# Delta rule: states decayed by ScalarE ahead of time, update products added four heads at once

## The chip, the cores and the metric

One core of one Trainium2 chip runs the kernel. The metric is device time in microseconds (us) of one execution. Engines are named by the profile's letters where rows are meant: PE is TensorE, DVE is VectorE, ACT is ScalarE, POOL is GpSimd, SP is SyncE.

## The reference, cut to what matters

The program computes two transformer-like blocks for 1024 tokens of width 1024. The change lies in the first block, in its bidirectional gated delta rule (4 heads, head size 128, chunks of 64 tokens, so 16 chunks in each direction). Per chunk and head a 128x128 state is read, and then replaced:

```python
def step(state, inp):
    q_i, k_i, u_i, w_i, g_i, a_i = inp
    v_new = u_i - jnp.einsum('bhcd,bhde->bhce', w_i, state)
    o = (jnp.einsum('bhcd,bhde->bhce', q_i * jnp.exp(g_i)[..., None], state)
         + jnp.einsum('bhcs,bhse->bhce', a_i, v_new))
    g_last = g_i[..., -1]
    k_dec = k_i * jnp.exp(g_last[..., None] - g_i)[..., None]
    state = state * jnp.exp(g_last)[..., None, None] + jnp.einsum('bhcd,bhce->bhde', k_dec, v_new)
    return state, o
```

The last but one line is what the change touches: the product of the state with its decay, and the addition of the update product.

## The kernel before, in words

The delta rule runs in one stage (`nc.Block(name="delta_and_window")`) together with the windowed attention of the same block. Both directions go side by side: forward chunk n and backward chunk 15 - n are one step n, each on half of the 128 partitions of a bank. `state` holds 8 states of 128x128 (4 heads, 2 directions) in SBUF; `chunk_decay` holds their decays, one number for each state and chunk.

**Periods and slots.** The order on every engine is written out by hand: the stage is a loop over periods s = 0 to 17, each of 10 slots k = 0 to 9. In a period, step n = s - 2 of the recurrence is done, and beside it parts of a triangular inverse for later chunks (`CHAIN`: `corner_sum`, `inv_sum` on TensorE with `corner_mask`, `inv_add` on VectorE). Of the recurrence in period s:

- slot 0: TensorE multiplies keys and queries with the old states (`state_sums`, L1203, 32 matmuls, into the banks `value_bank` and `kvb[0]`); ScalarE scales the second product (`q_state_scale`, L1382); VectorE subtracts the first (`subtract_state`, L1567).
- slot 4: TensorE forms v_new (`v_sum`, L1214), ScalarE copies it to SBUF (`v_copy`, L1391).
- slot 7: TensorE forms the update products of both directions (`kv_sum`, L1226, into `kvb[0]` and `kvb[1]`); VectorE replaces the states of one direction (`advance(z, 0)`, L1577).
- slot 8: output product (`out_sum`, L1235) and its addition on VectorE (`out_add`, L1585).
- slot 9: VectorE replaces the states of the other direction (`advance(z, 1)`, L1577) and posts the semaphore `s_st`, for which the next period's `state_sums` waits; then it takes up the next chunk (`scores_of`, L1514), whose product (`gram`, L1166) TensorE forms at the end of the period.

**The window attention** fills the slots 1 to 9 (from period 2, slot 4 on) with a running list of steps for 32 units u (`WINDOW_STEPS`): `score u+1`, `turn0 u`, `turn1 u`, `values u`, and again. Four kinds of steps over nine slots a period shift the list by one from period to period, so that slot 1 holds, period after period, `turn0`, `turn1`, `values`, `score`, `turn0`, and so on. In these steps TensorE transposes the probabilities of two heads through one bank `ptb` (L1288), ScalarE copies the first head's out (`copy_turned`, L1428), VectorE the second's (L1676); TensorE's `turn1` waits for ScalarE's copy. ScalarE also forms the probabilities of the next unit (`probs`, L1420) when slot `turn1` comes, and copies the values out of the last quarter of `ptb` after `values` (`copy_out`, L1433); TensorE's `turn0` of the next unit waits for that copy. `score` (L1274) needs no ScalarE instruction. In the last periods ScalarE has squares and scalings of finished outputs in the same slots (L1033, L1473).

Every engine works through its own list in order, so an instruction that waits holds up all behind it.

The function that the change alters, before:

```python
for h in range(DN_HEADS):
    j = d * 4 + h
    ins = nc.vector.scalar_tensor_tensor(state[:, j, :], state[:, j, :], chunk_decay[:, j, c:c + 1],
                                         kvb[hf][:, h, :], ALU.mult, ALU.add)
if hf:
    ins.then_inc(s_st, 1)
```

Of the kernel before, what the change touches and what calls it, by code (L numbers as in the profile page):

```python
# [10 lines left out]
ALU = mybir.AluOpType  # L11
ACT = mybir.ActivationFunctionType
# [11 lines left out]
DN_HEADS, DN_DIM, DN_TAPS, CH = 4, 128, 5, 64  # L24
NCH = SEQ // CH
# [111 lines left out]
def build(nc, t):  # L137

    ctx = ExitStack()
    with ctx:  # L140
        def sb(name, shape, dt=F32, where=ctx, side="left"):
            return where.enter_context(nc.sbuf_tensor(name, shape, dt, side=side))

        def bank(name, shape=(P, HALF), where=ctx):
            return where.enter_context(nc.psum_tensor(name, list(shape), F32))

        def sem(name):
            return ctx.enter_context(nc.semaphore(name))
# [155 lines left out]
        chunk_decay = sb("chunk_decay", [P, 8, NCH], F32, stDN)  # L304
# [48 lines left out]
        s_xturn, s_hhi, s_xcopy = sem("x_turned"), sem("h_hi_ready"), sem("x_copied")  # L353
        s_hlo = sem("h_lo_ready")
        s_sq, s_sqadd = sem("squares_ready"), sem("squares_added")
        s_ss, s_ln, s_rs = sem("square_sums"), sem("log_ready"), sem("rs_ready")
        s_tap, s_conv = sem("taps_step"), sem("conv_sum_ready")
        s_silu_free, s_zsilu = sem("tap_sum_free"), sem("gate_silu_done")
        s_resid_sp = sem("resid_spilled")
# [26 lines left out]
        with blockA as block:  # L386
# [304 lines left out]
            def _(dve):  # L691
# [106 lines left out]
                for c in range(C1):  # L798
# [44 lines left out]
                    elif c == 24:  # L843
# [15 lines left out]
        late = const("late").rearrange("p (r n) -> p r n", r=2)  # L859
        LEVELS, LOWER = 6, CH // 2  # L860
        PAIR_BUFS, INV_BUFS = 4, 3
        pair_keys = sb("pair_keys", [P, PAIR_BUFS, DN_HEADS, 2, CH], F32, stS)
        k_dec = sb("k_dec", [P, 2, DN_HEADS, DN_DIM], F32, stS)
        corner = sb("corner", [P, LEVELS, DN_HEADS, CH], F32, stS)
# [4 lines left out]
        state = sb("state", [P, 8, DN_DIM], F32, stS)  # L869
        tri = [bank(f"tri{i}", where=stS) for i in range(2)]  # L870
        value_bank = bank("value_bank", (P, DN_HEADS, DN_DIM), stS)
        kvb = [bank(f"kvb{i}", (P, DN_HEADS, DN_DIM), stS) for i in range(2)]
# [35 lines left out]
        s_vsum, s_vnew, s_osum, s_kv, s_st, s_o = (sem("v_new_summed"), sem("v_new_then_parts_taken"), sem("out_summed"),  # L908
                                                   sem("kv_summed"), sem("state_ready"), sem("out_stored"))
# [17 lines left out]
        def side(n, hf):  # L927

            return (n, 0) if hf == n % 2 else (NCH - 1 - n, 1)
# [26 lines left out]
        def chain_step(s, k):  # L956

            kind, behind, lv = CHAIN[k]
            n = s - behind
            return (kind if 0 <= n < NCH else None), n, lv  # L960

        corners, masks, sums_done, inverses = 0, 1, 0, 2
        for s in range(PERIODS):
            for k in range(SLOTS):
                kind, n, lv = chain_step(s, k)
# [17 lines left out]
        def window_step(s, k):  # L983

            return STEP_AT.get(s * SLOTS + k, (None, 0))
# [58 lines left out]
        with nc.Block(name="delta_and_window") as block:  # L1044
# [321 lines left out]
            def _(act):  # L1366
# [10 lines left out]
                def q_state_scale(n):  # L1377
                    act.wait_ge(s_qssum, n + 1)
                    if n >= 2:
                        act.wait_ge(s_o, 2 * n - 2)  # L1380
                    for h in range(DN_HEADS):
                        ins = nc.scalar.activation(q_state[:, n % 2, h, :], ob[:, h, :], ACT.Copy,  # L1382
                                                   scale=g_exp[:, n, h:h + 1])
                    ins.then_inc(s_qs, 1)

                def v_copy(n):
                    act.wait_ge(s_vsum, n + 1)
                    if n:
                        act.wait_ge(s_kv, n)
                        act.wait_ge(s_osum, n)  # L1390
                    nc.scalar.activation(v_new[:, :, :], value_bank[:, :, :], ACT.Copy).then_inc(s_vnew, 1)  # L1391

                def square(u):
                    blk, h = norm_units[u]
                    if u == 0:
                        act.wait_ge(s_wconst, 32)
                    if u == 2:
                        act.wait_ge(s_qk, 32)
                    if u >= 2:
                        act.wait_ge(s_hsum, u - 1)  # L1400
                    nc.scalar.activation(head_sq[:, u % 2, :], qk[:, blk, h * HALF:(h + 1) * HALF], ACT.Square
                                         ).then_inc(s_hsq, 1)

                def head_scale(u):
                    act.wait_ge(s_hsum, u + 1)
                    if u >= 2:
                        act.wait_ge(s_hn, u - 1)
                    nc.scalar.activation(head_rs[:, u % 2, :], scb[:, 0, :], ACT.Ln, bias=eps[:, 0:1],
                                         scale=1.0 / HD).then_inc(s_hln, 1)
                    act.wait_ge(s_hln, u + 1)  # L1410
                    nc.scalar.activation(head_rs[:, u % 2, :], head_rs[:, u % 2, :], ACT.Exp, scale=-0.5
                                         ).then_inc(s_hrs, 1)

                def probs(u):
                    b, i = att_units[u]
                    n = len(key_tiles(i)) * P
                    act.wait_ge(s_nm, u + 1)
                    for hd in range(2):
                        part = prob[:, u % 2, hd, 0:n]
                        nc.scalar.activation(part, part, ACT.Exp, bias=max_neg[:, b, i, hd:hd + 1], scale=-1.0,  # L1420
                                             accum_out=row_sum[:, b, i, hd:hd + 1]).then_inc(s_pr, 1)

                def copy_turned(u):
                    n = len(key_tiles(att_units[u][1])) * P
                    act.wait_ge(s_pt, 2 * u + 1)
                    if u:
                        act.wait_ge(s_pv, u)
                    nc.scalar.activation(prob_t[:, 0, 0:n], ptb[:, 0:n], ACT.Copy).then_inc(s_pta, 1)  # L1428

                def copy_out(u):  # L1430
                    b, i = att_units[u]
                    act.wait_ge(s_pv, u + 1)
                    nc.scalar.activation(y_ch[:, b, i * P:(i + 1) * P], pvb, ACT.Copy).then_inc(s_oc, 1)  # L1433

                def in_slot(s, k):
                    i = s * SLOTS + k - PREP_FROM
                    if i == 0:
                        square(0)
                        square(1)
                    if 0 <= i < NN:  # L1440
                        head_scale(i)
                        if i + 2 < NN:
                            square(i + 2)
                    kind, u = window_step(s, k)
                    if (kind, u) == ("score", 0):
                        probs(0)
                    elif kind == "turn0":
                        copy_turned(u)
                    elif kind == "turn1" and u + 1 < NA:
                        probs(u + 1)  # L1450
                    elif kind == "values":
                        copy_out(u)
# [33 lines left out]
                for s in range(PERIODS):  # L1486
                    z = s - 2
                    for k in range(SLOTS):
                        if k == 0 and z >= 0:
                            q_state_scale(z)  # L1490
                        if k == 4 and z >= 0:
                            v_copy(z)
                        in_slot(s, k)
                        if k == 5 and s + 1 < NCH:
                            decay_exp(s + 1)
                        if (s, k) in SQUARES_AT:
                            early_square(SQUARES_AT[s, k])
                        if (s, k) in ROOTS_AT:
                            early_roots(ROOTS_AT[s, k])
                        for n in SCALED_AT.get((s, k), ()):  # L1500
                            early_scaled(n)
                        if (s, k) == (NCH, 8):
                            act.wait_ge(s_den, 1)
                            nc.scalar.activation(sink_exp[:, :, :, :], sink_exp[:, :, :, :], ACT.Exp).then_inc(s_den, 1)
                        if k == 5 and z == NCH - 1:
                            copy_rows()

            @block.vector
            def _(dve):
# [61 lines left out]
                def advance(n, hf):  # L1571

                    dve.wait_ge(s_kv, n + 1)
                    c, d = side(n, hf)
                    for h in range(DN_HEADS):
                        j = d * 4 + h
                        ins = nc.vector.scalar_tensor_tensor(state[:, j, :], state[:, j, :], chunk_decay[:, j, c:c + 1],  # L1577
                                                             kvb[hf][:, h, :], ALU.mult, ALU.add)
                    if hf:
                        ins.then_inc(s_st, 1)  # L1580

# [124 lines left out]
                for s in range(PERIODS):  # L1706
                    z = s - 2
                    if s == 1:
                        small_vectors()
                    for k in range(SLOTS):  # L1710
                        kind, n, lv = chain_step(s, k)
# [2303 lines left out]
```

## Time and profile before

| | |
|---|---|
| runs (us) | 2014.56, 2015.43, 2016.87 |
| median of the runs (us) | 2015.43 |
| span of the profiled execution (us) | 2018.0 (its time is listed by this span alone) |
| stage of the delta rule in the span | about 340 to 672 us |
| periods 4 to 15 of it | about 18 us each |
| PE, DVE, ACT, POOL busy over the whole span | 97%, 67%, 41%, 18% |

The profile is of one execution, and the rows below have times from its start. A row of a timeline says when an instruction, or a run of equal ones (xN), began, how long it took, its engine, its line in the kernel, and in brackets how long the engine had been idle before it and what ended the wait. The rows PEld are TensorE's weight loads, which overlap its matmuls.

### The profile page before, as it was taken

The page shows a single profiled execution, that of the slowest core. Times are in us where ns is not written, and L with a number is a line of the kernel's source. Part 1 is how long each engine was busy: PE and PEld are TensorE (multiplying, and loading weights), DVE is VectorE, ACT ScalarE, POOL GpSimd, SP SyncE. Part 2 cuts the span into 40 slices and gives each one's busy share as a digit, 9 for nine tenths or more (in the row PEclk, how much of TensorE's full clock was granted, in tenths as well). Part 3 has the DMA queues.
Part 4 walks back from the last instruction along what each step waited for, and adds up shares of the span by engine and source line. Part 5 has one row for each costly group of instructions (what it writes and reads, how often), then busy time and mean ns, then how long its engine had stood idle before and what let it go on. Part 6 is the DMA issues. An engine that isn't in the chain of part 4 may idle for free. (4 is left out here: it accounts for less than half of the span.)

```text
span 2018.0 us, 34115 instructions
## 1 busy us (share of the span) xinstructions
PE 1957.7 (97%) x13859; PEld 1541.6 (76%) x13875; DVE 1348.2 (67%) x2152; ACT 819.4 (41%) x1536; POOL 369.5 (18%) x313
## 2 busy tenths in 40 slices
PE   7999999999999899999999999999999999999998
PEld 5888887577777687787676666787888888888886
DVE  5675323777776677664443566458988888877886
ACT  5112322443354436122222676345444444444342
POOL 3000001322333445011120362541000000000000
PEclk9999999999999899999999999999999999999999
DMA  6112324000000766831221220523322222269553
GB/s 216 53 52 73 103 85 147 9 3 2 3 3 2 266 194 203 326 114 33 63 85 63 111 79 2 167 84 136 105 78 90 84 74 94 84 225 348 193 193 136
DMA packets 192288, 220.79 MB, mean 109 GB/s; under 512 B 14240, under 2 KB 142212, under 8 KB 191492
## 3 DMA queue, kind: packets, MB, share of 16 engines
q1 hardware_dynamic: 182558, 190.68, 28.6%
q0 software_dynamic: 4640, 17.30, 2.2%
q10 hardware_dynamic: 4934, 10.61, 1.4%
q8 instruction: 111, 1.82, 0.4%
q14 instruction: 45, 0.37, 0.1%
HBM read 176.63 MB, written 41.94 MB: 108 GB/s over the span
## 5 line engine op out<-in xcount | busy, mean ns | idle before, releaser
L229 ACT ACTIVATE w_hi<-w_stage 128x1024 fp32r<-128x1024 f32 x88 | 93.1, 1058 | 309.0 <-PE acc L265 124.6
L263 PE MATMUL mix_acc<-mix_hi,w_hi 128*128 128x512 f32 x416 | 170.0, 409 | 0.0
L237 DVE TENSOR_TENSOR w_lo<-w_stage,w_hi 128x1024 fp32r<-128x1024 f32 x88 | 111.2, 1264 | 83.1 <-ACT w_hi L229 83.1
L265 PE MATMUL mix_acc<-mix_hi,w_lo 128*128 128x512 f32 x416 | 162.7, 391 | 0.0
L264 PE MATMUL mix_acc<-m_lo,w_hi 128*128 128x512 f32 x416 | 162.1, 390 | 0.0
L263 PE MATMUL acc<-h_hi,w_hi 128*128 128x512 f32 x400 | 158.0, 395 | 0.0
L265 PE MATMUL acc<-h_hi,w_lo 128*128 128x512 f32 x400 | 156.8, 392 | 0.0
L264 PE MATMUL acc<-h_lo,w_hi 128*128 128x512 f32 x400 | 156.7, 392 | 0.0
L1819 PE MATMUL mix_acc<-mix_hi,w_hi 128*128 128x512 f32 x288 | 116.0, 403 | 6.7 <-DVE w_lo L237 4.1
L809 DVE TENSOR_TENSOR raw<-acc,y_tok 128x1024 f32<-128x1024 f32 (+1 forms) x27 | 33.1, 1225 | 133.1 <-PE acc L265 127.5
L1820 PE MATMUL mix_acc<-m_lo,w_hi 128*128 128x512 f32 x288 | 112.9, 392 | 0.0
L1821 PE MATMUL mix_acc<-mix_hi,w_lo 128*128 128x512 f32 x288 | 112.9, 392 | 0.0
L3738 DVE SCALAR_TENSOR_TENSOR hidden<-work,hidden_conv,hidden 128x1023 f32<-128x1023 f32 x76 | 97.2, 1279 | 0.9
L263 PEld LDWEIGHTS mix_acc<-mix_hi,w_hi 128*128 128x128 f32 x416 | 78.1, 188 | 24.4 <-issue 9.2
L3303 ACT ACTIVATE w_hi<-w_stage 128x512 fp32r<-128x512 f32 (+1 forms) x91 | 55.0, 611 | 90.4 <-PE late_bank L3431 18.9
L265 PEld LDWEIGHTS mix_acc<-mix_hi,w_lo 128*128 128x128 f32 x416 | 78.1, 188 | 17.2
L264 PEld LDWEIGHTS mix_acc<-m_lo,w_hi 128*128 128x128 f32 x416 | 78.3, 188 | 15.6 <-issue 1.0
L265 PEld LDWEIGHTS acc<-h_hi,w_lo 128*128 128x128 f32 x400 | 75.8, 189 | 16.2
L264 PEld LDWEIGHTS acc<-h_lo,w_hi 128*128 128x128 f32 x400 | 75.9, 190 | 15.7
L263 PEld LDWEIGHTS acc<-h_hi,w_hi 128*128 128x128 f32 x400 | 75.8, 189 | 15.4
L1819 PEld LDWEIGHTS mix_acc<-mix_hi,w_hi 128*128 128x128 f32 x288 | 54.5, 189 | 22.7 <-DVE w_lo L237 5.2
L3591 ACT ACTIVATE hidden<-work,hidden_conv 128x1024 f32<-128x1024 f32 x38 | 47.3, 1246 | 48.4 <-DVE work L3842 47.8
(523 smaller groups left out, 5026.2 us busy)
## 6 DMA issues: line engine op xcount, KB each, us to landing
w_stage<-in_w_in SPq DMA_DIRECT2D x48, 512.0 KB, 4.4
w_stage<-in_w_up SPq DMA_DIRECT2D x44, 512.0 KB, 4.6
w_stage<-in_w_out SPq DMA_DIRECT2D x32, 512.0 KB, 3.7
w_ada<-in_w_ada SPq DMA_DIRECT2D x32, 512.0 KB, 5.0
w_stage<-in_w_down SPq DMA_DIRECT2D x14, 1024.0 KB, 5.5
a_stage<-hidden_spill SPq DMA_DIRECT2D x12, 1024.0 KB, 6.7
hidden_spill<-hidden SPq DMA_DIRECT2D x22, 512.0 KB, 2.6
spill<-y_tok POOLq DMA_DIRECT2D x20, 512.0 KB, 5.1
```

Source lines behind the costliest of these rows:

```text
L229: nc.scalar.activation(w_hi[:, slot], w_stage[:, slot], ACT.Copy).then_inc(w_hi_ready, 1)
L237: nc.vector.tensor_tensor(lo, w_stage[:, slot, 0:lo.shape[1]], hi.bitcast(F32), ALU.subtract).then_inc(w_lo_ready, 1)
L263: nc.tensor.matmul(acc[:, h, :], w_hi[:, slot, k, :], hi[:, k, tok], start=k == 0, stop=False)
L264: nc.tensor.matmul(acc[:, h, :], w_hi[:, slot, k, :], lo[:, k, tok], start=False, stop=False)
L265: mm = nc.tensor.matmul(acc[:, h, :], w_lo[:, slot, k, :], hi[:, k, tok], start=False, stop=k == kts - 1)
L809: nc.vector.tensor_tensor(raw[rows_used, c % 2, 2:SEQ + 2], acc[c % 2][rows_used, :, :].rearrange("p a b -> p (a b)"), rs[rows_used, :], A ...
L1819: nc.tensor.matmul(dst, w_hi[:, slot, k, :], hi[:, k, tok], start=u == 0, stop=False)
L1820: nc.tensor.matmul(dst, w_hi[:, slot, k, :], lo[:, k, tok], start=False, stop=False)
L1821: mm = nc.tensor.matmul(dst, w_lo[:, slot, k, :], hi[:, k, tok], start=False, stop=u == KT - 1)
L3303: nc.scalar.activation(ring(q % RING)[0][:, 0:nk], src, ACT.Copy).then_inc(w_hi_ready, 1)
L3591: nc.scalar.activation(hidden[:, f % 2, part, :], whole[:, part, :], ACT.Identity, bias=hidden_conv[:, 3, up:up + 1], scale=hidden_conv[:, ...
L3738: nc.vector.scalar_tensor_tensor(dst[:, d:], src[:, :SEQ - d], hidden_conv[:, k, up:up + 1], dst[:, d:], ALU.mult, ALU.add).then_inc(s_dta ...
```

## The change

ScalarE multiplies all eight states in place by their decays, in eight instructions of 128x128, in slot 1 of the periods 2 to 16 (the states have been read by `state_sums` by then, which `q_state_scale` in slot 0 has waited for). VectorE's `advance` then only adds the four update products of a direction, in one instruction of 128x512 in place of four of 128x128. It waits for a count on the semaphore `s_rs`, used earlier in the kernel for another purpose and standing at 2.

```diff
-        s_ss, s_ln, s_rs = sem("square_sums"), sem("log_ready"), sem("rs_ready")
+        s_ss, s_ln, s_rs = sem("square_sums"), sem("log_ready"), sem("rs_then_states_decayed")
...
+        DECAYED0, DECAY_SLOT = 2, 1
...
+                def decay_states(n):
+
+                    if n:
+                        act.wait_ge(s_st, n)
+                    for hf in range(2):
+                        c, d = side(n, hf)
+                        for h in range(DN_HEADS):
+                            j = d * 4 + h
+                            ins = nc.scalar.activation(state[:, j, :], state[:, j, :], ACT.Copy,
+                                                       scale=chunk_decay[:, j, c:c + 1])
+                        ins.then_inc(s_rs, 1)
...
                         in_slot(s, k)
+                        if k == DECAY_SLOT and 0 <= z < NCH - 1:
+                            decay_states(z)
...
                     dve.wait_ge(s_kv, n + 1)
+                    dve.wait_ge(s_rs, DECAYED0 + 2 * n + hf + 1)
                     c, d = side(n, hf)
-                    for h in range(DN_HEADS):
-                        j = d * 4 + h
-                        ins = nc.vector.scalar_tensor_tensor(state[:, j, :], state[:, j, :], chunk_decay[:, j, c:c + 1],
-                                                             kvb[hf][:, h, :], ALU.mult, ALU.add)
+                    both = state[:, d * 4:d * 4 + 4, :]
+                    ins = nc.vector.tensor_tensor(both, both, kvb[hf][:, :, :], ALU.add)
                     if hf:
                         ins.then_inc(s_st, 1)
```

(`act` and `dve` are the instruction lists of ScalarE and VectorE; lines behind the insertion have numbers higher by 1 to 15 in the changed kernel.)

ScalarE's list in period 10, whose slot 1 holds a `score` step, before (`window_region` is the tile of probabilities, `y_tok` receives the values):

```order
L1382 ACTIVATE q_state<-kvb,scales 128x128 x4
L1428 ACTIVATE window_region<-ptb 128x384
L1420 ACTIVATE window_region,row_sum<-window_region,max_neg 128x384 x2
L1391 ACTIVATE v_new<-value_bank 128x512
L1433 ACTIVATE y_tok<-ptb 128x128
```

The same place of ScalarE's list in the changed kernel:

```order
L1383 ACTIVATE q_state<-kvb,scales 128x128 x4
L1395 ACTIVATE state<-state,chunk_decay 128x128 x8
L1441 ACTIVATE window_region<-ptb 128x384
L1433 ACTIVATE window_region,row_sum<-window_region,max_neg 128x384 x2
L1404 ACTIVATE v_new<-value_bank 128x512
L1446 ACTIVATE y_tok<-ptb 128x128
```

The eight decays stand directly ahead of the copy of the first head's transposed probabilities, in this period and in periods 6 and 14.

ScalarE's list in period 16, whose slot 1 holds `turn1`, before (`qk` receives the squares of finished outputs, `mod` their sums):

```order
L1382 ACTIVATE q_state<-kvb,scales 128x128 x4
L1420 ACTIVATE window_region,row_sum<-window_region,max_neg 128x256 x2
L1433 ACTIVATE y_tok<-ptb 128x128
L1033 ACTIVATE qk,mod<-conv_in 128x128 x4
L1428 ACTIVATE window_region<-ptb 128x256
L1391 ACTIVATE v_new<-value_bank 128x512
```

The same place in the changed kernel:

```order
L1383 ACTIVATE q_state<-kvb,scales 128x128 x4
L1433 ACTIVATE window_region,row_sum<-window_region,max_neg 128x256 x2
L1395 ACTIVATE state<-state,chunk_decay 128x128 x8
L1446 ACTIVATE y_tok<-ptb 128x128
L1034 ACTIVATE qk,mod<-conv_in 128x128 x4
L1441 ACTIVATE window_region<-ptb 128x256
L1404 ACTIVATE v_new<-value_bank 128x512
```

Here the decays stand ahead of the copy of the values, and all that follows is behind them; the order of the other instructions is unchanged.

## Rows read from the trace of the kernel before

**Rows 1.** The page: TensorE's busy time, share of the span and instructions.

```profile
PE 1957.7 (97%) x13859; PEld 1541.6 (76%) x13875; DVE 1348.2 (67%) x2152; ACT 819.4 (41%) x1536; POOL 369.5 (18%) x313
```

**Rows 2.** Waits of TensorE, 399 to 646 us: total, times, longest.

```profile
PE tri L1166 <- DVE inv L1556: 2.8, 4, 0.8
PE ptb L1297 <- DVE window_region L1676: 2.4, 7, 0.5
PE kvb L1226 <- ACT pair_keys L1373: 2.4, 5, 0.6
```

**Rows 3.** Timeline, end of period 8 and start of period 9, VectorE and TensorE.

```profile
515.62 1.12 DVE L1577 SCALAR_TENSOR_TENSOR state<-state,chunk_decay,kvb 128x128 f32<-128x128 f32 x4
515.64 1.09 PE L1166 MATMUL tri<-conv_in 128*64 128x128 f32 x16
...
516.78 0.69 DVE L1514 TENSOR_TENSOR pair_keys<-tri,pair_keys 128x512 f32<-128x512 f32 x1
...
517.25 1.09 PE L1203 MATMUL value_bank<-state,conv_in 128*64 128x128 f32 x16
...
519.15 0.66 PE L1176 MATMUL tri<-inv,pair_keys 64*64 64x32 f32 x16
```

**Rows 4.** Timeline, starts of periods 16 and 17: state products, and what follows the first.

```profile
646.35 1.65 PE L1203 MATMUL value_bank<-state,conv_in 128*64 128x128 f32 x16 [1.12 <-DVE state L1577]
...
649.63 0.77 PE L1288 MATMUL ptb<-const_base,window_region 128*128 128x128 f32 x3
...
661.58 1.09 PE L1203 MATMUL value_bank<-state,conv_in 128*64 128x128 f32 x16 [1.85 <-DVE state L1577]
```

**Rows 5.** Groups by line, 340 to 690 us: count, busy us, mean ns, idle before.

```profile
L1577 DVE SCALAR_TENSOR_TENSOR state<-state,chunk_decay,kvb 128x128 f32<-128x128 f32 x120 | 33.6, 343 | 6.4 <-PE kvb L1226 5.7
...
L1585 DVE TENSOR_TENSOR q_state<-value_bank,q_state 128x512 f32<-128x512 f32 x15 | 10.3, 690 | 4.8 <-PE value_bank L1235 4.7
...
L1473 ACT ACTIVATE conv_in<-conv_in,mod 128x128 f32<-128x128 f32 x24 | 7.6, 400 | 0.0
```

**Rows 6.** Timeline, ScalarE in period 16: eight scalings of 128x128 in place.

```profile
659.02 2.43 ACT L1473 ACTIVATE conv_in<-conv_in,mod 128x128 f32<-128x128 f32 x8
```

**Rows 7.** Timeline, period 10: ScalarE's copy, and TensorE's transposes that wait for it.

```profile
536.83 1.14 ACT L1382 ACTIVATE q_state<-kvb,scales 128x128 f32<-128x128 f32 x4 [3.17 <-PE kvb L1203]
...
539.32 0.49 ACT L1428 ACTIVATE window_region<-ptb 128x384 f32<-128x384 f32 x1 [1.34 <-PE ptb L1288]
...
539.95 0.52 PE L1288 MATMUL ptb<-const_base,window_region 128*128 128x128 f32 x3
```

**Rows 8.** Timeline, period 16: end of the probabilities, copy of values, next transposes.

```profile
651.25 0.52 ACT L1420 ACTIVATE window_region<-window_region,max_neg 128x256 f32<-128x256 f32 x1
...
651.98 0.28 ACT L1433 ACTIVATE y_tok<-ptb 128x128 f32<-128x128 f32 x1
...
652.40 0.41 PE L1288 MATMUL ptb<-const_base,window_region 128*128 128x128 f32 x2 [0.47 <-ACT y_tok L1433]
```

**Rows 9.** Timeline, period 12 (slot 1 holds turn1): last probabilities, next transposes.

```profile
577.47 0.62 ACT L1420 ACTIVATE window_region<-window_region,max_neg 128x384 f32<-128x384 f32 x1
...
581.03 0.55 PE L1288 MATMUL ptb<-const_base,window_region 128*128 128x128 f32 x3
```

**Rows 10.** Timeline, period 9 (slot 1 holds values): copy of values, second transposes.

```profile
520.65 0.28 ACT L1433 ACTIVATE y_tok<-ptb 128x128 f32<-128x128 f32 x1 [0.25 <-PE ptb L1297]
...
524.20 0.44 PE L1288 MATMUL ptb<-const_base,window_region 128*128 128x128 f32 x2
```

**Rows 11.** Timeline, period 11 (slot 1 holds turn0): ScalarE's waits before v_copy.

```profile
559.61 0.28 ACT L1433 ACTIVATE y_tok<-ptb 128x128 f32<-128x128 f32 x1 [1.52 <-PE ptb L1297]
...
561.10 0.60 ACT L1391 ACTIVATE v_new<-value_bank 128x512 f32<-128x512 f32 x1 [1.21 <-PE value_bank L1214]
```

**Rows 12.** Stretches: length, busy PE, PEld, DVE, ACT, POOL; PEclk, DMA share, GB/s.

```profile
647.00:648.00 1.00, 1.00 (x13) 1.00 (x11) 0.00 (x0) 0.00 (x0) 0.00 (x0) 0.50 0.00 0
...
671.00:672.00 1.00, 0.00 (x0) 0.00 (x0) 0.73 (x2) 0.00 (x0) 0.00 (x0) 1.00 1.02 399
...
675.00:676.00 1.00, 1.00 (x5) 0.64 (x4) 0.13 (x1) 0.00 (x0) 1.00 (x2) 0.50 0.96 373
```

## The prediction

> **What bounds the kernel now.** The page comes first: TensorE is busy for 97% of the span [rows 1], so a change off TensorE can gain only where TensorE stands still. The waits of TensorE in the middle of the stage come next (13 periods): 2.8 us for the inverse on VectorE, 2.4 us for VectorE's copy of probabilities, 2.4 us for ScalarE's exponentials [rows 2]. No row there names the states. The timeline says why: `advance(z, 1)` starts at 515.62 beside `gram`, which starts at 515.64 and takes 1.09; `scores_of`, next on VectorE, starts at 516.78, when both have just ended, and the state products follow at 517.25, half a microsecond after the states are ready [rows 3]. A faster `advance` would leave VectorE waiting for `gram`, to the same moment. The two waits on VectorE in rows 2 start from work that TensorE feeds, not from `advance`: the inverse stands behind the masked scores of slot 8, the copy behind `scores_of` or `out_add`. Only at the starts of periods 16 and 17, where no `gram` stands between, does TensorE wait for the states: 1.12 and 1.85 us [rows 4].
>
> **The addition on VectorE.** Four instructions of `advance` take 1.12 us [rows 3]. No row has the new addition, but `out_add` has its form, 128x512 with one operand in a bank, at 0.69 [rows 5]; that is the value, and the bounds are 0.69 and 1.12, since one instruction cannot well cost more than four of the same elements. It saves 0.43 us, 30 times, 13 us of VectorE. On the path it counts twice, before periods 16 and 17: **minus 0.86 us** (bounds 0 and 0.9). The other 28 are covered by `gram` in slot 9 and, in slot 7, by `out_sum` and the attention's products; were that cover gone, they would give at most 12 us, which rows 2 exclude. The wait for the decays queues nothing: they are done in slot 3 at the latest, `advance` comes in slots 7 and 9. No DMA and no POOL instruction is moved.
>
> **The decays on ScalarE.** The nearest rows are eight scalings of 128x128 in place with a per-partition factor: 2.43 us together [rows 6], one lasting 0.40 [rows 5], so (2.43 - 0.40) / 7 = 0.29 from one start to the next, and 8 x 0.29 = 2.32 us by which ScalarE's next instruction is put off. Lower bound four `q_state` scalings at 1.14 [rows 7], 2.28 for eight; upper bound eight without overlap, 8 x 0.40 = 3.2. What is late behind them depends on what the period has in slots 1 to 4:
>
> - `turn0` in slot 1 (periods 3, 7, 11, 15): ScalarE idles 1.52 and 1.21 us up to `v_copy`, 2.73 in all [rows 11]; 2.32 fits. Cost 0.
> - `values` in slot 1 (5, 9, 13): the decays start at about 520.9, end 523.2; the copy of 0.5 us at most behind them ends at 523.7, and TensorE needs it at 524.20 [rows 10]. Cost 0.
> - `turn1` in slot 1 (4, 8, 12): the probabilities end at 578.09; 2.32 for the decays and 0.28 for the copy of values make 580.7; the next transposes are due at 581.03 [rows 9]. Cost 0, with 0.3 us to spare.
> - `score` in slot 1 (6, 10, 14): nothing of the attention separates `q_state` from the decays. ScalarE had 1.34 us idle before the copy at 539.32 [rows 7], so the copy comes 2.32 - 1.34 = 0.98 us late. `turn1` started 0.14 after the copy ended (539.81 and 539.95), and some of that is slack: 0.84 to 0.98. I take 0.85, three periods alike: **plus 2.55 us** (bounds 2.4 for decays as quick as `q_state`, 5.2 without overlap).
> - Period 16 has `turn1` in slot 1 too, but it is the last unit: no `score` follows, and the next transposes come a slot earlier. TensorE already waits 0.47 us for the copy of values [rows 8]. ScalarE ends its probabilities at 651.77 and starts that copy at 651.98, so 0.2 is idle at most and the copy comes 2.32 - 0.2 = 2.1 late: **plus 2.1 us** (2.1 to 3.0).
>
> TensorE works in order, so `v_sum`, `kv_sum` and the next period are behind each of these four waits; none is followed by a wait with slack that could take them up, because VectorE and ScalarE are fed by the products that are late. TensorE is 97% busy afterwards [rows 1], so the end moves with them.
>
> A page of the Trainium skill speaks against this part: "ScalarE: Activation LUTs", section "Rules for kernel authors", sends multiplications and additions to VectorE, not to ScalarE. The rows agree as to work: VectorE did both in one pass and saves 0.86 us a period, ScalarE pays 2.32. By the rule alone each of 15 periods would lose the difference, 22 us; the rows put the price on the path in four. That is the fourth rival.
>
> **The clock.** After the wait of 1.12 us at the start of period 16 the granted clock is 0.50 [rows 12], that is 1.2 GHz: two groups of state products take 649.63 - 646.35 = 3.28 us instead of 519.15 - 517.25 = 1.90 at 2.4 GHz [rows 3, 4], a loss of 1.4. The wait of 1.85 us before period 17 is followed by products of 1.09, full clock [rows 4]; after the idle time around 671 the clock is again 0.50 [rows 12]. So of three idle stretches above 1 us two were followed by the low clock. The change makes one of 0.47 + 2.1 = 2.6 us in period 16. I take the low clock after it: **plus 1.4 us** (bounds: minus 1.4, if the clock also stays up before period 16, and plus 1.4).
>
> **Sum.** 2.55 + 2.1 - 0.86 + 1.4 = 5.2 us. The profiled execution's span of 2018.0 becomes 2023.2. That execution lies 2.6 us above the median of the runs, 2015.43, so the median becomes 2020.6. A measurement of this kernel can tell some 0.2% from no change, 4.0 us; the forecast is **slower**, by little.
>
> **Rivals.**
>
> 1. *The new idle time is not followed by the low clock*, all else as forecast: 3.8 us, 2019.2, just within 0.2%. For it: the 1.85 us before period 17 [rows 4]. Chance 0.27.
> 2. *Not slower: the shorter wait keeps the clock up.* TensorE's wait before period 16 shrinks from 1.12 to 0.69, the state products stay at 2.4 GHz, and the new idle time too passes without loss: 3.8 - 1.4 = 2.4 us, 2017.8, within 0.2%. It decides whether TensorE's clock reads 1.00 in the microseconds after that wait. For it: shorter waits, of up to 0.8 us, occur before that in the stage [rows 2], and products as at 517.25 run at full clock [rows 3]. Against it: the idle time of period 16 is longer than any here. Chance 0.15.
> 3. *The decays don't overlap*, 3.2 us each time: the three periods cost 1.73 each, period 16 costs 3.0, and with the clock 5.2 + 3.0 - 0.86 + 1.4 = 8.7 us, 2024.1. Against it: rows 6 are the same form. Periods 4, 8 and 12 would lose their 0.3 of slack as well. Chance 0.06.
> 4. *ScalarE becomes the bound of every period* (the rule above): 15 x (2.32 - 0.86) = 22 us, 2037. It would need `v_copy` late in every period; ScalarE's 2.73 us of idle time [rows 11] speak against it. Chance 0.02.
> 5. *VectorE sets the pace*, and the time saved on it returns: the two waits on VectorE in rows 2, 5.2 us, with the 0.86 make 6 us, and the copies turn out early enough after all: 2009. Against it: rows 3. Chance 0.03.
>
> That the change does nothing is not open: a `state` instruction of ScalarE stands in each of 15 periods.
>
> **How the numbers follow.** The forecast itself has 0.47. Slower by over 0.2% takes four fifths of it, a third of rival 1 (0.2 us under the bound), rivals 3 and 4, and nothing else: 0.38 + 0.09 + 0.08 = 0.55, and 0.56 with a little of rival 2. Faster is rival 5 and hardly more: 0.03. Within 0.2%: 0.41. The range goes from 2017.0 (rival 2 with the decays at their lower bound and the runs' spread of 2.3 us in mind) to 2024.1 (rival 3); it leaves out rivals 4 and 5 and the tails.
>
> **What would show it.** Right: rows of eight decays of about 2.4 us on ScalarE, additions of 0.69 on VectorE; in periods 6, 10 and 14 TensorE's second transposes waiting about 0.85 us for ScalarE's copy; in period 16 a wait of about 2.6 us for the copy of values; waits of 0.7 and 1.4 us before periods 16 and 17; the other periods as long as before. Wrong: waits for ScalarE in periods with `turn0`, `turn1` or `values` in slot 1 (rivals 3, 4), periods that shorten by more than 0.1 us (rival 5), a granted clock of 1.00 from period 16 on (rivals 1, 2). Most likely to fail is the clock, since it was read from three cases.

## The result, and the profile after

The changed kernel takes 2028.26 us, the median of four runs (2023.62 to 2031.15); the kernel before takes 2014.99 beside it (2014.53 to 2016.87). The ratio is 1.0059, interval 1.0041 to 1.0077: 8 to 16 us slower. The forecast was plus 5.2 us, 2020.6, with a range up to 2024.1. Slower was right; the size was not. The profiled execution (span 2021.8, time 2023.62) is the quickest of the four.

**The pieces came as forecast.** Groups by line of the changed kernel, 340 to 690 us (count, busy us, mean ns, idle before):

```profile
L1395 ACT ACTIVATE state<-state,chunk_decay 128x128 f32<-128x128 f32 x120 | 36.6, 396 | 0.0
L1592 DVE TENSOR_TENSOR state<-state,kvb 128x512 f32<-128x512 f32 x30 | 20.6, 688 | 8.3 <-PE kvb L1227 7.5
```

The addition takes the 0.69 us of its model and one decay the 0.40 of its own [rows 5]; eight decays in a row take 2.44 (below), against 2.43 [rows 6]. Waits of TensorE in the changed kernel, 376 to 690 us (in total, times, longest):

```profile
...
PE ptb L1289 <- ACT window_region L1441: 2.8, 3, 0.9
PE ptb L1289 <- ACT y_tok L1446: 2.8, 1, 2.8
PE tri L1167 <- DVE inv L1571: 2.8, 4, 0.8
PE kvb L1227 <- ACT pair_keys L1374: 2.4, 5, 0.6
PE value_bank L1204 <- DVE state L1592: 2.3, 2, 1.6
```

The same view of the kernel before:

```profile
PE value_bank L1203 <- DVE state L1577: 3.0, 2, 1.8
...
PE tri L1166 <- DVE inv L1556: 2.8, 4, 0.8
...
PE kvb L1226 <- ACT pair_keys L1373: 2.4, 5, 0.6
...
PE ptb L1288 <- ACT y_tok L1433: 0.5, 1, 0.5
```

TensorE's transposes wait longer for ScalarE in four periods: three new waits for the copy of turned probabilities (periods 6, 10, 14; up to 0.9 each), and in period 16 the wait for the copy of the values, which grew from 0.5 to 2.8. The waits for the states shrank from 3.0 to 2.3. The others shown stand where they stood, so no other period waits longer for ScalarE than before.

**Period 16 holds most of the loss.** Its timeline in the changed kernel, TensorE and ScalarE, from one group of state products to the next (start, length, idle time before in brackets); the rows of before are [rows 4, 8]:

```profile
645.64 1.09 PE L1204 MATMUL value_bank<-state,conv_in 128*64 128x128 f32 x16 [0.68 <-DVE state L1592]
...
649.66 2.44 ACT L1395 ACTIVATE state<-state,chunk_decay 128x128 f32<-128x128 f32 x8
651.99 0.26 ACT L1446 ACTIVATE y_tok<-ptb 128x128 f32<-128x128 f32 x1
...
652.40 0.66 PE L1289 MATMUL ptb<-const_base,window_region 128*128 128x128 f32 x2 [2.79 <-ACT y_tok L1446]
...
653.87 1.95 PE L1215 MATMUL value_bank<-v_rest,inv 64*64 64x128 f32 x16
...
665.23 1.09 PE L1204 MATMUL value_bank<-state,conv_in 128*64 128x128 f32 x16 [1.57 <-DVE state L1592]
```

Stretches of the same time, columns as in [rows 12]:

```profile
646.00:648.00 2.00, 2.00 (x33) 1.68 (x29) 1.13 (x4) 0.34 (x2) 0.10 (x1) 1.00 0.03 8
650.00:652.00 2.00, 0.00 (x0) 0.00 (x0) 0.00 (x0) 2.00 (x9) 0.00 (x0) 1.00 0.00 0
653.00:657.00 4.00, 3.48 (x37) 2.75 (x36) 0.72 (x2) 1.29 (x6) 1.03 (x1) 0.50 0.00 0
657.00:661.00 4.00, 4.00 (x40) 3.39 (x40) 0.74 (x2) 1.95 (x11) 1.04 (x1) 0.50 0.00 0
661.00:662.00 1.00, 1.00 (x20) 0.99 (x20) 0.82 (x2) 0.02 (x1) 0.00 (x0) 0.50 0.00 0
664.00:668.00 4.00, 2.77 (x37) 2.13 (x37) 2.72 (x9) 1.33 (x5) 2.53 (x2) 1.00 0.08 7
```

Two things are to be seen. From 646 to 648 the granted clock is 1.00, where before it was 0.50, that is 1.2 GHz, from 647 to 648 [rows 12]: the state products take 1.09 us instead of 1.65 [rows 4]. And after the wait that ends at 652.4 it is 0.50 for some ten microseconds, though TensorE is hardly idle in them (4.00 of 4.00 us busy from 657 to 661): the 16 products of v_new take 1.95 us, while the same product takes 1.07 at full clock. The forecast priced this stretch at 1.4 us.

### The profile page after: what moved, and what is told of

Same layout as the page of the kernel before. It is cut to its first block and busy times, and to the rows that moved or that the text cites. A ratio compares the mean times of both kernels' runs of the same rounds, so it can differ in the third digit from the quotient of the medians.

```text
span 2021.8 us, 34191 instructions
## 1 busy us (share of the span) xinstructions
PE 1964.1 (97%) x13875; PEld 1543.6 (76%) x13875; DVE 1335.8 (66%) x2062; ACT 853.2 (42%) x1656; POOL 370.5 (18%) x313
## 5 line engine op out<-in xcount | busy, mean ns | idle before, releaser
L263 PEld LDWEIGHTS acc<-h_hi,w_hi 128*128 128x128 f32 x400 | 75.4, 188 | 15.5
```

What stands on the lines that cost most here:

```text
L263: nc.tensor.matmul(acc[:, h, :], w_hi[:, slot, k, :], hi[:, k, tok], start=k == 0, stop=False)
```

## The experiments

All rows of experiments were read as those above: "up to period 16" is the time from the first state products of the stage to those of period 16, "period 16" from there to those of period 17. Each start is a row of the timeline; for the changed kernel the first is

```profile
375.96 1.09 PE L1204 MATMUL value_bank<-state,conv_in 128*64 128x128 f32 x16
```

so up to period 16 it takes 645.64 - 375.96 = 269.68 us, and period 16 takes 665.23 - 645.64 = 19.59. For the kernel before it is

```profile
380.11 1.09 PE L1203 MATMUL value_bank<-state,conv_in 128*64 128x128 f32 x16
```

and up to period 16 it takes 646.35 - 380.11 = 266.24. "0.50 within" gives the starts of stretches at the half clock, from these first state products to the end of period 17, and their lengths; they are read from one profiled execution of each kernel. "To before" is the ratio to the runs of the kernel before beside it, over all executions, put in us, with its interval.

| kernel | up to period 16 | period 16 | 0.50 within (us) | to before (us) |
|---|---|---|---|---|
| before | 266.24 | 15.23 | 646: 3.4 | |
| before, again | 266.26 | 15.20 | 644: 3.4 | +1.4 (-0.4 to 3.0) |
| the change | 269.68 | 19.59 | 563: 3.4; 652: 10.2 | +11.9 (8.3 to 15.5) |
| the change, again | 268.10 | 19.40 | 652: 17.1 | +10.7 (7.9 to 13.7) |
| the change, third | 269.65 | 19.62 | 566: 3.4; 655: 10.2 | one run |
| decays placed | 265.63 | 13.06 | none | -2.0 (-4.6 to 0.4) |
| decays placed, again | 265.65 | 13.06 | none | -2.2 (-4.8 to 0.2) |
| periods 6, 10, 14 mended | 265.63 | 19.69 | 650: 10.2 | +3.0 (1.4 to 4.8) |
| period 16 mended | 269.65 | 13.06 | 497: 3.4 | +2.2 (0 to 4.6) |
| period 16 filled | 269.83 | 15.38 | 494: 3.4 | +4.0 (1.0 to 6.9) |
| all four filled | 269.78 | 15.37 | 566: 3.4 | +4.6 (1.8 to 7.5) |
| ScalarE's part alone | 268.55 | 19.89 | 653: 17.1 | +13.9 (11.3 to 16.7) |
| VectorE's part alone | 265.63 | 13.05 | none | -1.8 (-3.6 to -0.2) |
| placed, and filled | 265.64 | 13.24 | none | 0.0 (-3.2 to 3.2) |
| before, 1.0 us later | 268.93 | 15.21 | 485: 3.4; 648: 3.4 | one run |
| before, 2.1 us later | 268.20 | 13.63 | 661: 3.4 | one run |

**1. The change, again.** No edit.

> The changed kernel unaltered, for more executions and a second profile. Theory A (low clock): the four waits of TensorE for ScalarE cost 4.7 us by themselves, and the rest of the 13 us is TensorE's low clock that they bring; executions then spread over several us (2022 to 2032), the long ones with the lower mean granted clock, and a second profile shows stretches at 0.50 at other places of the stage than the first. Theory B (a fixed cost outside the rows read): the executions agree within 3 us, and the profile's stage is as long as in the first.

Measured: 2026.73 us (2023.7 to 2032.18) against 2016.47, ratio 1.0053 (1.0039 to 1.0068). The loss is there in a second series. Single executions spread over 8 us, as theory A had it; the profile has its half clock behind the same wait of period 16, for longer, and the stretch at 563 is missing.

**2. The decays placed where nobody waits for them**: in slot 2 in periods 6, 10 and 14, and behind the copy of v_new in period 16.

```diff
-                        if k == DECAY_SLOT and 0 <= z < NCH - 1:
+                        if k == (4 if s == 16 else 2 if s in (6, 10, 14) else DECAY_SLOT) and 0 <= z < NCH - 1:
```

> Decays moved in periods 6, 10 and 14 behind the copy of slot 2, in period 16 behind v_copy of slot 4; nothing else changed. Theory A: no wait for ScalarE is left, so the loss goes altogether, and the shorter wait for the states remains: 0.9 us below the kernel before, up to 2.5 below with the clock up at period 16; 2012 to 2015. Theory B (the cost lies in ScalarE's extra 37 us of work or in VectorE's new instruction wherever it stands): the loss of about 13 us remains.

Measured: 2013.47 us, ratio 0.999 (0.9977 to 1.0002). Its waits of TensorE, 376 to 690 us:

```profile
PE ptb L1298 <- DVE window_region L1690: 2.9, 8, 0.5
PE tri L1167 <- DVE inv L1571: 2.8, 4, 0.8
...
PE kvb L1227 <- ACT pair_keys L1374: 2.3, 5, 0.6
PE value_bank L1204 <- DVE state L1592: 2.3, 2, 1.6
...
PE ptb L1289 <- ACT y_tok L1446: 0.5, 1, 0.5
```

The three waits for turned probabilities are gone, the one for the values is back at the 0.5 that it had before, and with them the whole loss is gone. All 120 decays and 30 additions are still there, so their work costs nothing by itself; four places did.

**3. and 4. One half of that each**: slot 2 in periods 6, 10 and 14 alone, then the later place in period 16 alone.

```diff
-                        if k == DECAY_SLOT and 0 <= z < NCH - 1:
+                        if k == (2 if s in (6, 10, 14) else DECAY_SLOT) and 0 <= z < NCH - 1:
```

> Only periods 6, 10 and 14 mended; period 16 as in the change. Theory A with the low clock mostly after period 16's wait: about 2.6 us less than the change, 2025, with about 10 us at clock 0.50 in periods 16 and 17. If the low clock comes mostly from the waits of periods 6, 10, 14: 2019 to 2021.

```diff
-                        if k == DECAY_SLOT and 0 <= z < NCH - 1:
+                        if k == (4 if s == 16 else DECAY_SLOT) and 0 <= z < NCH - 1:
```

> Only period 16 mended; the waits in periods 6, 10 and 14 as in the change. Theory A with the low clock mostly after period 16's wait: 2016 to 2018, that is 2.6 us of waits less 0.9 to 2.3. If the low clock comes mostly from the waits of periods 6, 10, 14: 2020 to 2024, with stretches at 0.50 between 450 and 640 us.

Measured: 2020.49, ratio 1.0015 (1.0007 to 1.0024), with the three periods mended; 2019.45, ratio 1.0011 (1.0 to 1.0023), with period 16 mended. In the profiled periods of the table the three periods cost 269.65 - 265.63 = 4.0 us, and period 16 costs 19.69 - 13.06 = 6.6. The whole times are another matter: beside the same runs of the kernel before, mending the three periods alone gains 10.7 - 3.0 = 7.7 us, mending period 16 alone 8.5, and both together 12.7, so there the halves do not simply add. Theory A was missed in both: 2020.49 lies far under its 2025, in the range given for a half clock that comes mostly from the three periods, and 2019.45 lies between the two ranges given.

**5. The kernel before, again**, as a measure of what can be told apart.

> The kernel before, for its granted clock in each execution and a second profile. Theory A (the loss is waits plus the low clock that they bring): a mean granted clock of 0.992 to 0.995, above the 0.986 to 0.992 of the change, and no stretch at 0.50 of more than 4 us at the start of period 16. Theory B (the clock wanders by itself and the change only lengthens the stage): the same clock as the change.

Measured: 2017.28 against 2016.46, ratio 1.0007 (0.9998 to 1.0015). Single runs of it reach from 2014.04 to 2022.52. The granted clock, averaged over a whole execution, is 0.991 to 0.995 here; it is 0.986 to 0.992 in the ten executions of the change (result and experiment 1), on average 0.989 against 0.993. The half clock is part of the loss, then, as theory A says. With either half mended (experiments 3 and 4) the average is 0.992 and 0.993, so most of the additional half clock went with either; why is not shown.

**6. The wait of period 16 filled.** Twelve multiplications that nobody reads stand ahead of the transposes that wait. ScalarE's list is untouched, so the values come as late as in the change.

```diff
+                        if (s, k) == (NCH, 3):
+                            keep_busy(tri[0][:, :], 12)
```

> The change, with 12 idle matmuls (2.6 us) on TensorE ahead of the transposes of period 16, where it waits for ScalarE: the wait stays as long, but TensorE works through it. Theory A: no long stretch at 0.50 in periods 16 and 17, so 4 to 6 us less than the change, 2021 to 2023. Theory C (the wait itself is the loss, and the low clock beside it costs little): as the change, 2026 to 2028.

Measured: 2020.79, ratio 1.002 (1.0005 to 1.0034). Its timeline and then its stretches in period 16:

```profile
651.96 1.09 PE L1204 MATMUL value_bank<-state,conv_in 128*64 128x128 f32 x16 [0.69 <-DVE state L1594]
...
655.87 2.76 PE L285 MATMUL tri<-const_base 128*128 128x512 bf16 x12
658.73 0.41 PE L1289 MATMUL ptb<-const_base,window_region 128*128 128x128 f32 x2
...
659.55 1.07 PE L1215 MATMUL value_bank<-v_rest,inv 64*64 64x128 f32 x16
```

```profile
658.00:660.00 2.00, 1.91 (x29) 1.24 (x29) 0.23 (x1) 2.00 (x12) 0.00 (x0) 1.00 0.00 0
660.00:662.00 2.00, 1.48 (x22) 0.99 (x18) 0.48 (x2) 0.62 (x2) 1.21 (x2) 1.00 0.00 0
662.00:664.00 2.00, 2.00 (x44) 1.75 (x41) 0.85 (x3) 1.74 (x10) 0.86 (x1) 1.00 0.00 0
```

This parts the wait from the clock. The transposes start as late as in the change (6.8 us after the state products in both), but the clock stays at 1.00, and period 16 takes 15.38 instead of 19.59 us. So the wait is 15.38 - 13.06 = 2.3, and the half clock behind it costs **4.2 us**. The Trainium skill, "TensorE: Matmul & The Clock Gate", section "HAM oscillation — how this bites in real kernels", puts the penalty at half of the throttled time. That would be an estimate of 5.1 for 10.2 us; the measured 4.2 lie below it. Part of the stretch is idle time, such as the 0.52 us for which TensorE waits for VectorE in both kernels, and it gets no longer at the half clock. By the whole times the fill gains about 7 us, more than these 4.2, and the mean granted clock of its nine executions is 0.992.

**7. and 8. The two halves of the change apart.** First ScalarE's instructions, the semaphore and VectorE's wait, but with a factor of one, and VectorE's four old instructions; then VectorE's addition alone, without the decays.

```diff
-                                                       scale=chunk_decay[:, j, c:c + 1])
+                                                       scale=ones[:, 0:1])
...
-                    both = state[:, d * 4:d * 4 + 4, :]
-                    ins = nc.vector.tensor_tensor(both, both, kvb[hf][:, :, :], ALU.add)
+                    for h in range(DN_HEADS):
+                        j = d * 4 + h
+                        ins = nc.vector.scalar_tensor_tensor(state[:, j, :], state[:, j, :], chunk_decay[:, j, c:c + 1],
+                                                             kvb[hf][:, h, :], ALU.mult, ALU.add)
```

> Only ScalarE's half: its eight multiplications at the places of the change, but by one; VectorE multiplies and adds as before, in four instructions. Theory A: the waits for ScalarE and their low clock as in the change, and the longer wait for the states as before: 2026 to 2031, up to 2.5 us above the change. If VectorE's new form is what costs, it is as before, 2016.

```diff
-                        if k == DECAY_SLOT and 0 <= z < NCH - 1:
-                            decay_states(z)
...
-                    dve.wait_ge(s_rs, DECAYED0 + 2 * n + hf + 1)
```

> Only VectorE's half: one addition of 128x512 per direction, and no multiplication by the decay anywhere (the kernel leaves it out, so its results are others). Theory A: the waits for the states before periods 16 and 17 fall by 0.43 us each and the clock stays up after the first: 1 to 3 us below before, as with the decays placed without waits (2013.5). If placing alone made that run fast, or the VectorE part gives nothing: 2016.

Measured: 2029.58, ratio 1.0069 (1.0056 to 1.0083), for ScalarE's part; 2014.26, ratio 0.9991 (0.9982 to 0.9999), for VectorE's. The whole loss is ScalarE's. VectorE's part is worth about 2 us, at the edge of what can be told, and as much in the placed kernels. The table says where from: 266.24 - 265.63 = 0.6 us ahead of period 16, and 15.23 - 13.05 = 2.2 in it, since the half clock after its state wait is gone.

**9. All four waits filled.**

```diff
+                        if (s, k) == (NCH, 3):
+                            keep_busy(tri[0][:, :], 12)
+                        if k == 3 and s in (6, 10, 14):
+                            pe.wait_ge(s_vr, z + 1)
+                            keep_busy(value_flat, 4)
```

> The change, with small multiplications that fill TensorE's idle time at all four places: 12 of them ahead of the third slot of period 16, and 4 each ahead of the third slot's wait in periods 6, 10 and 14. The waits for ScalarE stay as they are (2.8 us in the three periods, 2.8 us in period 16); only TensorE's idle time in them is filled. Theory A (the waits cost their own time, and the half clock that follows them costs the rest): about 3 to 5 us over the kernel before, 2016 to 2021 us, 1 to 4 us under the run with period 16 alone filled. Theory B (the clock in periods 6, 10 and 14 has nothing to do with the waits): within 1 us of the run with period 16 alone filled, ratio about 1.002.

Measured: 2022.36, ratio 1.0023 (1.0009 to 1.0037). The idle time of the transposes in periods 6, 10 and 14 is gone from TensorE's rows, and nothing is won: 269.78 us up to period 16, 269.83 without this fill. Theory B holds here. A stretch at 0.50 comes in period 11 again, two dozen microseconds after the filled wait of period 10.

**10. and 11. The placed kernel once more, and with fills in periods 16 and 17.**

```diff
-                LAST_FILL = {0: 5, 4: 4, 8: 8}
+                LAST_FILL = {0: 5, 4: 4, 8: 14}
...
+                        if k == 0 and z >= NCH - 2:
+                            pe.wait_ge(s_oadd, z)
+                            keep_busy(value_flat, 3 if z == NCH - 2 else 6)
...
-                        if k == DECAY_SLOT and 0 <= z < NCH - 1:
+                        if k == (4 if s == 16 else 2 if s in (6, 10, 14) else DECAY_SLOT) and 0 <= z < NCH - 1:
```

> The change with the decays moved where nobody waits for them (second slot in periods 6, 10 and 14, behind the copy of the values in period 16), a second sample of it. Theory A: 1 to 3 us under the kernel before, ratio 0.998 to 1.000. Theory B (there is nothing in the addition on VectorE that is worth time, and the first sample was spread): ratio 1.000 or above.

> The decays moved where nobody waits for them, and small multiplications in TensorE's idle time of periods 16 and 17: ahead of the state products (3 and 6) and ahead of the third slot of period 16 (8). Theory A (the half clock behind the remaining waits, 6.8 us at 0.50 from 667 in the placed kernel, costs time that filling brings back): 1 to 4 us under the placed kernel, ratio to the kernel before 0.996 to 0.999. Theory B (the half clock is then drawn by something else, or the fill itself delays the products behind it): same as the placed kernel within 1 us, or slower.

Measured: 2014.06, ratio 0.9989 (0.9976 to 1.0001), and 2016.75, ratio 1.0 (0.9984 to 1.0016). The second sample repeats the first. The second kernel differs from what its expectation says: the 8 multiplications ahead of the third slot of period 16 are not in it, and slot 8 of period 17 has 14 in place of 8. The fill is a miss: the stretch at 0.50 after 667 became shorter (3.4 us instead of 6.8), but the stage is no shorter for it, and period 16 is 0.2 longer. No version that computes the result beats the kernel before by more than can be told: the placed ones lie about 2 us under it, at the edge.

**12. to 14. The kernel before with everything later by 1.0 and 2.1 us, and the change a third time.** In the first two, 4 and 8 multiplications stand in period 4 (the diff shows the first); the semaphore that they wait for has been posted by then, so TensorE does not stand still there:

```diff
+                        if (s, k) == (4, 3):
+                            pe.wait_ge(s_vr, z + 1)
+                            keep_busy(value_flat, 4)
```

> The kernel before, with 4 dense multiplications of 128x512 (1.04 us) put into period 4 of the stage, so that all that follows comes about 1 us later; no wait is added. Theory A (the low clock at half a microsecond's idle time in period 11, seen in three of the changed kernels, depends on when in the run that place falls, not on the waits for ScalarE): a stretch of 3.4 us at 0.50 can turn up in periods 8 to 13 here too, where the kernel before had none in two profiles. Theory B (it takes the waits of periods 6, 10 and 14): the granted clock reads 1.00 from period 5 to the start of period 16. Time: 1 to 2 us over the kernel before by B, up to 4 by A.

> The same with 8 multiplications (2.1 us). Theory A: as above, a low stretch in periods 8 to 13 can turn up; if it does in one of the two and not in the other, the place in time decides. Theory B: 1.00 from period 5 to the start of period 16 in both.

> The change unaltered, a third profile. Period 16's wait of 2.8 us for the copy of values stays. Theory A (the length of the low clock behind it changes from one execution to the next, with the moment at which the wait falls): 10 or 17 us at 0.50 from about 652, as in the two profiles there are, and a low stretch in period 11 in some executions only. Theory B (length and place belong to the kernel): the same as in one of the two, 0.50 in period 11 included.

Measured, one run each: 2021.55, 2020.67 and 2031.62, against 2015.52. The first two are 6.0 and 5.2 us over that single run, more than either expectation gave; single runs spread by more. Stretches of the kernel that is 1.0 us later:

```profile
484.00:485.00 1.00, 0.54 (x16) 0.42 (x15) 1.00 (x3) 0.12 (x2) 0.00 (x0) 1.00 0.00 0
485.00:488.00 3.00, 3.00 (x38) 2.67 (x40) 0.75 (x3) 0.28 (x1) 0.00 (x0) 0.51 0.00 0
488.00:489.00 1.00, 1.00 (x12) 0.83 (x10) 0.00 (x0) 0.13 (x1) 0.08 (x1) 0.76 0.00 0
```

Here the clock falls in the middle of the stage, with no decay and none of the four longer waits for ScalarE, after half a microsecond of idle time that the kernel before has too. The kernel that is 2.1 us later has no such stretch, and it lacks the one at 646 too: its period 16 takes 13.63. So theory B falls: the new waits are not needed for such a stretch. That the shift brought it about is not shown, since each kernel was profiled once. The third profile of the change has 10.2 us in period 16, as the first had; the second had 17.1; the stretch in the middle of the stage is there in the first and the third and not in the second. The length behind the same wait changes from one execution to the next.

## Why the prediction was right in its sign and wrong in its size

**The waits: right.** The decays were priced at 2.32 us, with four places where somebody waits for them. Up to period 16 the profile of experiment 1, which has no stretch at 0.50 there, takes 268.10 against 265.63 of the placed kernel: 2.5 us for the three periods, where 2.55 was forecast. Period 16's wait is 2.3, where 2.1 was forecast. The other periods show no longer wait for ScalarE, the one with 0.3 us to spare included; experiment 2 shows that these four places are all.

**The addition: right.** State waits of 0.68 and 1.57 us stand where 1.12 and 1.85 stood [rows 4]: 0.72 less, where 0.86 was forecast; the 28 other additions are worth nothing that the waits show, as argued from [rows 3].

**The clock: the step that failed.** The prediction put it so: "I take the low clock after it: plus 1.4 us (bounds: minus 1.4, if the clock also stays up before period 16, and plus 1.4)". That the half clock follows the new wait was right, in all five profiles that have this wait unfilled; the size was off. The price was carried over from the stretch of 3.4 us after the state wait [rows 12], which is followed by two groups of state products. In its place the runs showed three terms:

- plus 4.2 behind the wait of period 16 (experiment 6), three times the price taken;
- minus 1.9 at the start of period 16, where the clock stays up after the shorter wait: 15.23 - 13.06 = 2.2 in all, of which 0.3 is the shorter wait before period 17. The kernel that is 2.1 us later keeps the longer wait and has the clock up, and its period 16 takes 13.63, so the clock accounts for about 1.6 of the 1.9. Of five profiles with the wait of 1.12 us three show the half clock behind it, of ten with 0.68 none. That is the first half of rival 2; its second half, that the new idle time passes without loss, fell;
- plus 1.6 in period 11 (269.68 against 268.10), by a stretch that five of seven profiles with the decays in slot 1 of periods 6, 10 and 14 have somewhere between 494 and 570 us (after 0.6 to 0.8 us of idle time in period 7 or 11, before the update products), and one of nine others.

Net, the clock took about 4 us of this profile where 1.4 was priced. With 2.5 and 2.3 for the waits and about 0.9 less for the additions these make 7.8 us, the difference of 269.68 + 19.59 and 266.24 + 15.23. This agreement proves nothing more, since every term is a difference of rows of the same table. Rivals 3, 4 and 5 fell: eight decays take 2.44 us, and no period but these four got a longer wait for ScalarE.

One reading of the forecast was loose: it set the span of the profiled execution, 2018.0, against the times of runs, and a time is about 1.8 us longer than its span (2023.62 and 2021.8 in the changed kernel). The forecast of plus 5.2 us does not depend on it.

**What stays open.** The runs lie 8 to 16 us over the kernel before, the three profiles of the change 7.8, 6.0 and 7.8 over its first profile in these periods. The mean granted clocks of experiment 5 tell what the rest may be: 0.989 instead of 0.993 is some 17 us more at the half clock in an execution, of which the three profiles show 10 to 14 in these periods. At 4.2 us for 10.2 that is an estimate of 7 us for the clock, and with 3.9 for the waits and the additions (2.5 + 2.3 - 0.9) 11, near the 10.7 and 11.9 measured. Where the remaining half clock falls was not followed.

Single executions also differ ahead of the first decay. The first state products start between 375.96 and 385.21 us in the 16 profiles, and the latest start, in experiment 4, has this stretch before it (columns as in [rows 12]):

```profile
344.00:367.00 23.00, 22.53 (x142) 11.48 (x143) 10.07 (x23) 10.05 (x22) 1.32 (x2) 0.50 0.24 95
```

The kernel before starts them 4.15 us later than the change in the first profiles; so the two spans differ by only 3.8 us, less than the forecast, where the periods differ by 7.8.

From period 17 to the end of the span the kernel before takes 1356.4 and 1355.0 us in its two profiles, the change 1356.6, 1359.0 and 1361.2. In the second of these the 17.1 us at 0.50 reach past the start of period 17; for the rest no cause is shown, and single executions of other versions differ by as much (1354.8 to 1359.0). It was not tried whether the later start of the stages behind draws more of the half clock there. Nor is it settled why the stretch of period 11 comes with the waits so often: filling TensorE's idle time there did not remove it, and one of two shifted kernels had one without these waits. That the moment at which an idle place comes decides would fit both, but it is not shown.

## What to carry to other kernels

When work is moved to an engine with time to spare, count its slack period by period up to the next instruction that another engine waits for: here 120 instructions were free, but for the four places where the copy behind them was due at once, and another slot in those cost nothing. Price an idle stretch of TensorE by what follows it: a wait that grew from 0.5 to 2.8 us cost 2.3 us as a wait and 4.2 by the clock behind it, and idle multiplications in the wait gave back the latter. If forecasts rest on the clock, its bounds should take in stretches several times as long as the one that the profile happens to show.

## What the runs showed of the hardware that was not expected

A busy TensorE can stay at 1.2 GHz: from 653 to 662 us of the change it is busy for 8.5 of 9 us, and the granted clock is 0.50 throughout; in two other profiles the stretch behind this wait is 17.1 us long. At the start of the stage in experiment 4 it is busy for 22.53 of 23 us at 0.50, ahead of anything that the change does. After the wait at the start of period 16 in the kernel before, with its two groups of state products behind it, it was back after 3.4 us.

The same kernel can draw the half clock at one place in one execution and not in another: 3.4 us in period 11 of the change in its first and third profiles, none there in the second. Experiment 5's spread of single runs of the unchanged kernel, 8.5 us, is wider than most of the differences sought here.
